# Differential attention: the inner key product step is put between values and scores, the first scores wait for three parts, and weight splits are moved to the last heads

## The chip, the cores and the metric

The kernel runs on one core of a Trainium2 chip. The metric is the device time of one execution in microseconds (us). Three runs of the kernel before gave 1989.1, 1990.81 and 1990.58 us; the median is 1990.58.

## The reference, cut to what matters

The whole program is two transformer blocks on 512 tokens of width 1024. The part that the change touches is the differential attention of the second block:

```python
q = apply_rope(q, cos, sin)          # 8 heads, 2 components of 64
k = apply_rope(k, cos, sin)
s = jnp.einsum('bqhcd,bkhcd->bhcqk', qb, k) * scale      # causal
p = jax.nn.softmax(s, axis=-1)
a = p[:, :, 0] - lam * p[:, :, 1]
o = jnp.einsum('bhqk,bkhe->bqhe', a, v)                  # v: 128 wide
```

Beside it the program computes the first four column tiles of another product of the same normed input (`proj = h @ w_in`): raw keys and values of the compressed branch and the keys of two other branches. This is the "inner key product" here, stage `nsf`.

## The kernel before, in words

Every large product is made exact with three matmuls: high by high, high by low, low by high. Weights come in 512 KB chunks into six slots. For each chunk SyncE loads the raw floats, ScalarE casts them to the high part `Wh` (line 1324), VectorE writes the low part `Wl` over the raw floats (line 1834), and TensorE may then use it. These two instructions are a **weight split**. A chunk's slot comes free when TensorE is done with the chunk five or six places earlier, so a split may be made early or late within that span.

The attention stage has 32 tiles `t`: 8 heads of 4 query tiles each. Tile `t` belongs to head `t // 4`; with `t % 4` from 0 to 3 its scores are 512, 384, 256 and 128 keys wide, so the widest tile of a head comes first. The engines run written-out lists in order; they meet only at semaphores:

- **TensorE** (`attention`, line 893): `scores(0)`, `scores(1)`, eight inner product steps, and then for each `t`: `values(t-2)` (line 867: two matmuls for each 128 keys), `scores(t+2)` (lines 844 to 848, twice, for the components m = 0 and 1), `turn(t)` (line 857: transposes of the combined probabilities), and one inner product step where there is one (`nsf_step(t)`: every `t` below 27 but 0, 9, 18; three matmuls of 512 columns, lines 689 to 691). All inner steps add up in bank 7, a column tile being eight steps.
- **VectorE** (line 2043): for each `t`: `combine(t)` (lines 2036, 2038, 2040: both components of the exponentials into one, which lets `turn(t)` go), `maxima(t+2)` (line 2028, two reductions), and a split where `t` is in `LOW_AT`.
- **ScalarE** (line 1508): for each `t`: at t = 0, 9, 18, 27 `nsf_out` (line 1506: copies bank 7 out and so frees it), `da_out(t-2)` (line 1498, writes YD and frees bank 6 for the next `values`), `turned_out(t)` (line 1494: the transposed tile into ATd, for `values`), `exps(t+2)` (line 1485), at `t % 4` 3 and 0 a `q_high` (line 1533: high part of the next head's queries), and a split where `t` is in `HIGH_AT`.
- **GpSimd** (`qk_low`, line 558): for each head two casts (`Kh`, line 572) and four subtractions that write the low parts: `Kl` m = 0, `Kl` m = 1 (line 579), `Qst` m = 0, `Qst` m = 1 (line 587). Each subtraction adds one to `st_lo`; `scores` of a head's first tile waits for all four. They are fenced by `a_ready` of the head before, and the two last by `q_high`.

Banks 0 to 3 of PSUM hold scores, 4 and 5 transposes, 6 the output, 7 the inner product. At t = 29 to 31 `nst_tile` steps (304 columns wide) of the next product stand behind the turns.

Of the kernel before, what the change touches and what calls it, by code (L numbers as in the profile page):

```python
# [93 lines left out]
def at_least(eng, sem, value):  # L94

    if isinstance(value, int) and value <= 0:
        return
    eng.wait_ge(sem, value)


def program(nc, t, out, stop=None):
# [9 lines left out]
    with ExitStack() as ctx:  # L111
# [3 lines left out]
        def sem(name):  # L115
            return ctx.enter_context(nc.semaphore(name))
# [156 lines left out]
        for c, units in enumerate((3, 2, 2, 2, 3, 2, 2) * 2):  # L273
            s = len(GATE_AT)
            cuts = (0, 4, 8) if units == 2 else ((0, 3, 5, 8) if s % 2 else (0, 3, 6, 8))
            for n in range(units):
# [51 lines left out]
        st_lo = sem("st_lo")  # L328
# [50 lines left out]

        TWIN_AT = {CHUNK0["vda"] + 4: (0,), CHUNK0["vda"] + 7: (1,), CHUNK0["nsf"]: (2, 3), CHUNK0["nsf"] + 1: (4, 5),  # L380
                   CHUNK0["nsf"] + 2: (6, 7)}
        HIGH_AT = (1, 5, 9, 17, 25)
        LOW_AT = (5, 9, 13, 21, 29)

        def qk_parts(head):

            return 4 * head
# [5 lines left out]
        def nsf_ends(t):  # L393

            return t // 9 if t % 9 == 0 and t // 9 < 4 else None

        def nsf_step(t):

            return 8 + t - t // 9 - 1 if t % 9 and t < 27 else None
# [5 lines left out]
        def exists(t):  # L405

            return 0 <= t < TOTAL

        def tile_of(t):
            return 3 - t % 4  # L410

        def width(t):
            return (tile_of(t) + 1) * P
# [268 lines left out]
        def _(pe):  # L682
            def weights(k, it=0):

                pe.wait_ge(w_lo, it * 4 + (k + 1))
                return k % SLOTS

            def three(dst, a_hi, a_lo, b_hi, b_lo, start, stop):
                tensor.matmul(dst, a_hi, b_hi, start=start, stop=False)  # L689
                tensor.matmul(dst, a_hi, b_lo, start=False, stop=False)  # L690
                return tensor.matmul(dst, a_lo, b_hi, start=False, stop=stop)  # L691

            def bank_free(stage, b, k=0):
                at_least(pe, free[b], k + FREED[stage][b])
# [137 lines left out]
            def scores(t):  # L832
                i, u, b2 = tile_of(t), t // 4 % 2, 2 * (t % 2)
                w = width(t)
                q = slice(i * P, (i + 1) * P)
                if t % 4 == 0:
                    pe.wait_ge(st_lo, qk_parts(t // 4) + 4)
                    pe.wait_ge(k_twin[u], 32 * (t // 8) + 32)
                for m in range(2):
                    b = b2 + m  # L840
                    bank_free("da", b, t // 2)
                    dst = ps[b][:, 0:w]
                    if m == 1:
                        tensor.matmul(ps[b][:, w - P:w], identb[:], causal, start=True, stop=False, skip_group_check=True)
                    tensor.matmul(dst, Qst[:, u, m, q], Kh[:, u, m, 0:w], start=m == 0, stop=False, skip_group_check=m == 1)  # L845
                    last = tensor.matmul(dst, Qst[:, u, m, q], Kl[:, u, m, 0:w], start=False, stop=m == 1, skip_group_check=m == 1)
                    if m == 0:
                        last = tensor.matmul(ps[b][:, w - P:w], identb[:], causal, start=False, stop=True)
                    last.then_inc(full[b], 1)

            def turn(t):

                pe.wait_ge(a_ready, t + 1)
                b = 4 + t % 2
                bank_free("da", b, t // 2)
                for j in range(width(t) // P):
                    last = tensor.transpose(ps[b][:, j * P:(j + 1) * P], Pb2[:, t % 2, 0, j * P:(j + 1) * P], ident[:])
                last.then_inc(full[b], 1)

            def values(t):  # L860
                u, n = t % 2, tile_of(t) + 1
                b = 6
                bank_free("da", b, t)
                head = t // 4
                bank_free("da", 4 + u, t // 2 + 1)
                for j in range(n):
                    last = tensor.matmul(ps[b][:, 0:P], ATd[:, u, j * P:(j + 1) * P], vd[:, j, head * P:(head + 1) * P],  # L867
                                         start=j == 0, stop=j == n - 1)
                last.then_inc(full[b], 1)

            def nsf_steps(a, b):
                for n in range(a, b):
                    c, k = n // 8, n % 8
                    w = weights(CHUNK0["nsf"] + c)
                    if k == 0:
                        bank_free("nsf", 7, c)
                    q = slice(k * P, (k + 1) * P)
                    last = three(ps[7][:], Wh[:, w, q], Wl[:, w, q], HTh[:, k, :], HTl[:, k, :], k == 0, k == KT - 1)
                    if k == KT - 1:
                        last.then_inc(w_used, 1)  # L880

            def nst_tile(c, tt):
                s = weights(CHUNK0["nst"] + c)
                q = slice(tt * P, (tt + 1) * P)
                if c == 0:
                    bank_free("nst", tt)
                for j, k in enumerate(range(c * VG_K, min(c * VG_K + VG_K, KT))):
                    n = slice(j * VG_W, (j + 1) * VG_W)
                    last = three(ps[tt][:, 0:VG_W], HTh[:, k, q], HTl[:, k, q], Wh[:, s, n], Wl[:, s, n], k == 0, k == KT - 1)
                if tt == TT - 1:  # L890
                    last.then_inc(w_used, 1)

            def attention():
                scores(0)
                scores(1)
                nsf_steps(0, 8)
                for t in range(TOTAL):
                    if exists(t - 2):
                        values(t - 2)
                    if exists(t + 2):  # L900
                        scores(t + 2)
                    turn(t)
                    if nsf_step(t) is not None:
                        nsf_steps(nsf_step(t), nsf_step(t) + 1)
                    if t == TOTAL - 3:
                        nst_tile(0, 0)
                        nst_tile(0, 1)
                    if t == TOTAL - 2:
                        nst_tile(0, 2)
                        nst_tile(0, 3)  # L910
                    if t == TOTAL - 1:
                        nst_tile(1, 0)
                        nst_tile(1, 1)
                values(TOTAL - 2)
                nst_tile(1, 2)
                nst_tile(1, 3)
                values(TOTAL - 1)
# [175 lines left out]
            if on("da"):  # L1093
                pe.wait_ge(st_zero, 1)
                attention()
# [221 lines left out]
        def _(ac):  # L1317
# [8 lines left out]
            def chunk_done(stage, c, it=0):  # L1326
                ac.wait_ge(w_used, it * 4 + (CHUNK0[stage] + c + 1))

            def filled(stage, b, k=0):
                ac.wait_ge(full[b], k + (FILLED[stage][b] + 1))  # L1330
# [157 lines left out]
            def turned_out(t):  # L1488

                w = width(t)  # L1490
                u = t % 2
                filled("da", 4 + u, t // 2)
                at_least(ac, full[6], FILLED["da"][6] + t - 1)
                scalar.copy(ATd[:, u, 0:w], ps[4 + u][:, 0:w]).then_inc(free[4 + u], 1)
# [6 lines left out]
            def nsf_out(c):  # L1501
                chunk_done("nsf", c)
                if c >= 2:
                    ac.wait_ge(st_lo, qk_parts((4, 7)[c - 2]) + 4)
                dst = kcv[:, c, :] if c < 2 else kraw[:, c - 2, :]
                scalar.copy(dst, ps[7][:]).then_inc(free[7], 1)

            def attention():
                exps(0)
                exps(1)  # L1510
                for t in range(TOTAL):
                    if nsf_ends(t) is not None:
                        nsf_out(nsf_ends(t))
                    if exists(t - 2):
                        da_out(t - 2)
                    turned_out(t)
                    head = t // 4 + 2
                    if exists(t + 2):
                        exps(t + 2)
                    if t % 4 == 3 and head < 8:  # L1520
                        q_high(head, 0)
                    if t % 4 == 0 and 2 <= t // 4 + 1 < 8:
                        q_high(t // 4 + 1, 1)
                    if t in HIGH_AT:
                        split(CHUNK0["vda"] + 7 + HIGH_AT.index(t) + LEAD)
                da_out(TOTAL - 2)
                da_out(TOTAL - 1)
# [299 lines left out]
        def _(ve):  # L1827
# [215 lines left out]
            def attention():  # L2043
                maxima(0)
                maxima(1)
                for t in range(TOTAL):
                    combine(t)
                    if exists(t + 2):
                        maxima(t + 2)
                    if t in LOW_AT:  # L2050
                        split(CHUNK0["vda"] + 7 + LOW_AT.index(t) + LEAD)

# [583 lines left out]
```

## Time and profile before

| | |
|---|---|
| median of three runs | 1990.58 us |
| the profiled execution | 1989.57 us |
| its span | 1987.8 us |
| TensorE (matmul) busy | 1962.2 us, 99% |
| VectorE, ScalarE, GpSimd busy | 52%, 41%, 14% |
| chain of waits | 92% on TensorE |
| granted TensorE clock | full in all slices |

A time in a row counts from the start of the span. TensorE rows are matmuls: the start of one that follows a short matmul is shown up to 0.09 us early, and its end holds the drain of the array (0.16 us and more), so two starts are a better measure than one length. The square brackets say how long the engine sat idle before the row and who released it. Where equal instructions were merged, the row says how many.

### The profile page before, as it was taken

What the parts mean: (1) busy time and instruction counts of PE and PEld (TensorE: products, weight loads), DVE (VectorE), ACT (ScalarE), POOL (GpSimd) and SP (SyncE); (2) the same over time, 40 slices, a digit from 0 to 9 for tenths busy, and PEclk for the clock granted to TensorE, in tenths of its full rate; (3) what the DMA queues carried; (4) which work ended last, traced back from release to release, by engine and by line L of the source; (5) the groups of instructions that cost most, each with busy time, mean ns of one, the idle gap of its engine ahead of it and who ended that gap; (6) DMA issues with size and microseconds to landing.
All of it is one profiled execution on the core that took longest, in us unless ns stands there. A gap on an engine that the chain in (4) does not pass through costs nothing.

```text
span 1987.8 us, 25222 instructions
## 1 busy us (share of the span) xinstructions
PE 1962.2 (99%) x10000; PEld 1662.0 (84%) x10000; DVE 1029.9 (52%) x1575; ACT 805.4 (41%) x1466; POOL 269.6 (14%) x280
## 2 busy tenths in 40 slices
PE   8999999999999999999999999999999999999998
PEld 7888988888888888888988788888888888888887
DVE  6765665555354222333563768877765543222333
ACT  5542543334343222333333873566663342222332
POOL 1001000000000000000003542477860000000000
PEclk9999999999999999999999999999999999999999
DMA  6331333333323333332453144211225323333332
GB/s 213 106 100 56 112 107 102 98 96 96 96 88 107 101 98 96 96 96 85 122 151 114 50 149 148 73 61 49 64 78 198 112 79 110 98 96 95 96 96 74
DMA packets 60100, 201.68 MB, mean 101 GB/s; under 512 B 8304, under 2 KB 8336, under 8 KB 59600
## 3 DMA queue, kind: packets, MB, share of 16 engines
q1 hardware_dynamic: 56080, 185.10, 30.0%
q0 software_dynamic: 3904, 14.97, 2.2%
q8 instruction: 80, 1.31, 0.3%
q14 instruction: 36, 0.29, 0.1%
HBM read 180.64 MB, written 8.39 MB: 95 GB/s over the span
## 4 chain that ended last, share of the span: by engine, by line
PE 92%; DVE 3%; ACT 2%; POOL 1%; issue 1%; DVEq 1%; DMA 1%; POOLq 0%; ACTq 0%; SPq 0%
PE ps L691 27%; PE ps L689 27%; PE ps L690 27%; PE ps L1203 1%; PE ps L1241 1%; PE ps L1240 1%; PE ps L1183 1%; PE ps L1184 1%; PE ps L781 1%; PE ps L1110 1%; POOL PU L645 1%; DVE XN L1874 1%; PE ps L867 1%; ACT XN L1357 0%; PE ps L845 0%
## 5 line engine op out<-in xcount | busy, mean ns | idle before, releaser
L1834 DVE TENSOR_TENSOR Wl<-raw,Wh 128x1024 fp32r<-128x1024 f32 x307 | 378.3, 1235 | 688.9 <-ACT Wh L1324 687.5
L689 PE MATMUL ps<-HTh,Wh 128*128 128x512 f32 (+1 forms) x1712 | 641.4, 375 | 2.1 <-DVE gst L2416 1.2
L691 PE MATMUL ps<-HTh,Wl 128*128 128x512 f32 (+1 forms) x1712 | 636.8, 372 | 0.0
L690 PE MATMUL ps<-HTl,Wh 128*128 128x512 f32 (+1 forms) x1712 | 636.5, 372 | 0.0
L1324 ACT CAST Wh<-raw 128x1024 fp32r<-128x1024 f32 x307 | 321.7, 1051 | 736.1 <-DMA raw<-in_w_all 736.1
L691 PEld LDWEIGHTS ps<-HTh,Wl 128*128 128x128 f32 x1712 | 322.4, 188 | 56.3
L689 PEld LDWEIGHTS ps<-HTh,Wh 128*128 128x128 f32 x1712 | 322.6, 188 | 55.8 <-issue 2.1
L690 PEld LDWEIGHTS ps<-HTl,Wh 128*128 128x128 f32 x1712 | 322.7, 189 | 53.3
L689 PE MATMUL ps<-Wh,Yh 128*128 128x512 f32 x528 | 205.8, 390 | 0.0
L691 PE MATMUL ps<-Wh,Yl 128*128 128x512 f32 x528 | 205.5, 389 | 0.0
L690 PE MATMUL ps<-Wl,Yh 128*128 128x512 f32 x528 | 205.4, 389 | 0.0
L645 POOL TENSOR_SCALAR PU<-PU,ugg 128x512 f32<-128x512 f32 (+3 forms) x128 | 138.6, 1099 | 74.1 <-DVE ugg L2397 74.0
L689 PEld LDWEIGHTS ps<-Wh,Yh 128*128 128x128 f32 x528 | 99.1, 188 | 20.6
L690 PEld LDWEIGHTS ps<-Wl,Yh 128*128 128x128 f32 x528 | 99.1, 188 | 20.5
L691 PEld LDWEIGHTS ps<-Wh,Yl 128*128 128x128 f32 x528 | 99.1, 188 | 20.4
L689 PE MATMUL ps<-Wh,HTh 128*128 128x512 f32 (+1 forms) x288 | 110.7, 384 | 0.0
L691 PE MATMUL ps<-Wh,HTl 128*128 128x512 f32 (+1 forms) x288 | 109.4, 380 | 0.0
L690 PE MATMUL ps<-Wl,HTh 128*128 128x512 f32 (+1 forms) x288 | 109.3, 380 | 0.0
L1753 ACT ACTIVATE PU<-ps,umx 128x512 f32<-128x512 f32 (+3 forms) x128 | 65.9, 528 | 56.0 <-DVE umx L2389 56.0
L593 POOL MEMSET Kl<- 64x512 f32 x4 | 2.0, 522 | 453.6 <-DVE qkd L1943 453.6
L691 PEld LDWEIGHTS ps<-Wh,HTl 128*128 128x128 f32 x288 | 54.1, 188 | 10.1
L690 PEld LDWEIGHTS ps<-Wl,HTh 128*128 128x128 f32 x288 | 54.1, 188 | 9.7
(287 smaller groups left out, 2265.6 us busy)
## 6 DMA issues: line engine op xcount, KB each, us to landing
raw<-in_w_all SPq DMA_DIRECT2D x307, 512.0 KB, 3.5
swp_d<-qkd SPq DMA_DIRECT2D x64, 64.0 KB, 2.8
g_dram<-gst SPq DMA_DIRECT2D x16, 256.0 KB, 3.8
ring<-g_dram POOLq DMA_DIRECT2D x16, 256.0 KB, 3.5
X<-in_x SPq DMA_DIRECT2D x4, 512.0 KB, 6.2
swp_r<-qkr SPq DMA_DIRECT2D x16, 128.0 KB, 3.6
gpre<-in_g_pre POOLq DMA_DIRECT2D x4, 512.0 KB, 3.9
Kh<-Kh SPq DMA_DIRECT2D x16, 128.0 KB, 2.3
```

The lines of the kernel that those rows point to most:

```text
L645: last = pool.tensor_scalar(p, p, ugg[:, s % 2, i:i + 1], None, ALU.mult)
L689: tensor.matmul(dst, a_hi, b_hi, start=start, stop=False)
L690: tensor.matmul(dst, a_hi, b_lo, start=False, stop=False)
L691: return tensor.matmul(dst, a_lo, b_hi, start=False, stop=stop)
L781: last = tensor.transpose(ps[b][:, j * P:(j + 1) * P], XN[:, tt, k * P:(k + 1) * P], ident[:])
L867: last = tensor.matmul(ps[b][:, 0:P], ATd[:, u, j * P:(j + 1) * P], vd[:, j, head * P:(head + 1) * P], start=j == 0, stop=j == n - 1)
L1110: last = tensor.matmul(ps[kv][:, ht * 64:ht * 64 + 62], cw[:, j, ht * P:(ht + 1) * P], cA[:, kv, j, :], start=j == 0, stop=j == 15)
L1183: tensor.matmul(ps[b][:, o:o + w], q, ksh[:, m, g, 0:w], start=first, stop=False, skip_group_check=not first)
L1184: return tensor.matmul(ps[b][:, o:o + w], q, ksl[:, m, g, 0:w], start=False, stop=end, skip_group_check=not first)
L1324: scalar.copy(Wh[:, s, :], raw[:, s, :]).then_inc(w_hi, 1)
L1753: last = scalar.activation(PU[:, (s + 1) % 2, SCORE_AT[i]:SCORE_AT[i] + w], ps[b][:, o:o + w], ACT.Exp, bias=umx[:, s % 2, i:i + 1], accum ...
L1834: vector.tensor_tensor(Wl[:, s, :], raw[:, s, :], Wh[:, s, :], ALU.subtract).then_inc(w_lo, 1)
```

## The change

Four edits, all in the attention stage: on TensorE the inner step of `t` is issued before `scores(t+2)` and `turn(t)`; on ScalarE `nsf_out` is issued after `turned_out(t)`; the first tile of a head waits for three low parts ahead of component 0 and for the fourth ahead of component 1; and the five weight splits go to other tiles.

```diff
-        HIGH_AT = (1, 5, 9, 17, 25)
-        LOW_AT = (5, 9, 13, 21, 29)
+        HIGH_AT = (17, 21, 25, 27, 29)
+        LOW_AT = (18, 22, 26, 28, 30)
...
                 if t % 4 == 0:
-                    pe.wait_ge(st_lo, qk_parts(t // 4) + 4)
                     pe.wait_ge(k_twin[u], 32 * (t // 8) + 32)
                 for m in range(2):
                     b = b2 + m
+                    if t % 4 == 0:
+                        pe.wait_ge(st_lo, qk_parts(t // 4) + 3 + m)
                     bank_free("da", b, t // 2)
...
                     if exists(t - 2):
                         values(t - 2)
+                    if nsf_step(t) is not None:
+                        nsf_steps(nsf_step(t), nsf_step(t) + 1)
                     if exists(t + 2):
                         scores(t + 2)
                     turn(t)
-                    if nsf_step(t) is not None:
-                        nsf_steps(nsf_step(t), nsf_step(t) + 1)
...
                 for t in range(TOTAL):
-                    if nsf_ends(t) is not None:
-                        nsf_out(nsf_ends(t))
                     if exists(t - 2):
                         da_out(t - 2)
                     turned_out(t)
+                    if nsf_ends(t) is not None:
+                        nsf_out(nsf_ends(t))
                     head = t // 4 + 2
                     if exists(t + 2):
                         exps(t + 2)
```

## Rows read from the trace of the kernel before

**Rows 1.** Page, part 1: busy time, share of the span and instructions of each engine.

```profile
PE 1962.2 (99%) x10000; PEld 1662.0 (84%) x10000; DVE 1029.9 (52%) x1575; ACT 805.4 (41%) x1466; POOL 269.6 (14%) x280
```

**Rows 2.** TensorE's waits in 1080 to 1185 us: total, times, longest.

```profile
PE ps L867 <- ACT YD L1498: 1.5, 2, 1.3
PE ps L857 <- DVE Pb L2040: 1.5, 3, 0.7
PE ps L845 <- POOL Qst L587: 0.9, 3, 0.3
```

**Rows 3.** Windows: the ten us behind the stage (length, then busy of each engine).

```profile
1185.00:1195.00 10.00, 10.00 (x55) 8.81 (x54) 7.35 (x12) 9.84 (x20) 8.85 (x11) 1.00 0.90 320
```

**Rows 4.** Timeline of TensorE, one head: scores(16), scores(17), turn(16), values(16), scores(20).

```profile
1133.11 0.50 PE L845 MATMUL ps<-Kh,Qst 128*128 128x512 f32 x1 [0.29 <-POOL Qst L587]
...
1135.82 0.42 PE L845 MATMUL ps<-Kh,Qst 128*128 128x384 f32 x1
...
1138.86 0.66 PE L857 MATMUL ps<-ident,Pb 128*128 128x128 f32 x4
...
1142.15 1.16 PE L867 MATMUL ps<-vd,ATd 128*128 128x128 f32 x8
...
1143.45 0.50 PE L845 MATMUL ps<-Kh,Qst 128*128 128x512 f32 x1
```

**Rows 5.** Timeline of TensorE, start: scores(3), turn(1), values(0), scores(4).

```profile
1098.31 0.31 PE L845 MATMUL ps<-Kh,Qst 128*128 128x128 f32 x1
...
1098.80 0.28 PE L846 MATMUL ps<-Kl,Qst 128*128 128x128 f32 x1
1099.74 0.55 PE L857 MATMUL ps<-ident,Pb 128*128 128x128 f32 x3 [0.66 <-DVE Pb L2040]
...
1100.82 1.05 PE L867 MATMUL ps<-vd,ATd 128*128 128x128 f32 x8
1101.63 0.48 PE L845 MATMUL ps<-Kh,Qst 128*128 128x512 f32 x1
```

**Rows 6.** Timeline of ScalarE, start: nsf_out(0) and turned_out(0).

```profile
1097.50 0.59 ACT L1506 COPY kcv<-ps 128x512 f32<-128x512 f32 x1 [2.99 <-PE ps L691]
1098.59 0.59 ACT L1494 COPY ATd<-ps 128x512 f32<-128x512 f32 x1 [0.50 <-PE ps L857]
```

**Rows 7.** Timeline of ScalarE and TensorE at t = 9 and 10: nsf_out(1), da_out(7), values(8).

```profile
1120.71 0.59 ACT L1506 COPY kcv<-ps 128x512 f32<-128x512 f32 x1
1121.32 0.37 ACT L1498 ACTIVATE YD<-ps,rr 128x128 f32<-128x128 f32 x1
...
1121.74 1.16 PE L867 MATMUL ps<-vd,ATd 128*128 128x128 f32 x8 [1.31 <-ACT YD L1498]
```

**Rows 8.** Timeline of VectorE: combine(3); maxima(16) and combine(15); maxima(20).

```profile
1104.24 0.35 DVE L2040 SCALAR_TENSOR_TENSOR Pb<-Pb,gg 128x128 f32<-128x128 f32 x1
...
1133.95 1.29 DVE L2028 TENSOR_REDUCE nmx<-ps 128x1 f32<-128x512 f32 x2 [0.61 <-PE ps L848]
...
1135.74 0.88 DVE L2040 SCALAR_TENSOR_TENSOR Pb<-Pb,gg 128x128 f32<-128x128 f32 x1
...
1144.30 1.29 DVE L2028 TENSOR_REDUCE nmx<-ps 128x1 f32<-128x512 f32 x2 [2.03 <-PE ps L848]
```

**Rows 9.** Timeline of VectorE and GpSimd: two weight splits and a low part of queries.

```profile
1078.28 1.30 POOL L587 TENSOR_TENSOR Qst<-qkd,Qst 64x512 fp32r<-64x512 f32 x1 [0.16 <-issue]
1078.80 1.86 DVE L1834 TENSOR_TENSOR Wl<-raw,Wh 128x1024 fp32r<-128x1024 f32 x1 [4.73 <-ACT Wh L1324]
...
1120.18 1.22 DVE L1834 TENSOR_TENSOR Wl<-raw,Wh 128x1024 fp32r<-128x1024 f32 x1
1121.31 0.16 DVE L2036 RECIPROCAL rr<-rs 128x2 f32<-128x2 f32 x1
```

**Rows 10.** Timeline of TensorE, last head: turn(28) and turn(29).

```profile
1169.75 0.66 PE L857 MATMUL ps<-ident,Pb 128*128 128x128 f32 x4 [0.23 <-DVE Pb L2040]
...
1171.75 0.55 PE L857 MATMUL ps<-ident,Pb 128*128 128x128 f32 x3 [0.60 <-DVE Pb L2040]
```

## The prediction, written before any run of the changed kernel

> **What bounds the kernel now.** The page's first part comes first: TensorE is busy for 99% of the span, the others for about half or less [rows 1]. So a change of order can only win TensorE's idle time, or add to it. The windows behind the attention stage show it busy for 10.00 of 10 us [rows 3]; the matmul list there is fixed, so what the stage loses or gains goes to the end undiminished. The waits inside the stage are small and short: values for YD, turn for Pb, scores for Qst, 3.9 us together [rows 2]. Starts against starts tell more, since each wait also empties the array.
>
> Then the timeline of one head, read as a loop. scores(16) starts at 1133.11, turn(16) at 1138.86 (5.75 later), values(16) at 1142.15 (3.29 later), scores(20) at 1143.45 (1.30 later) [rows 4]. The first leg runs through VectorE: maxima(16) 0.84 behind the scores, combine(15), then maxima(17) and combine(16) [rows 4, 8]. The second runs through ScalarE: turned_out(16), exps(18), q_high, da_out(15), which frees bank 6. In the third, values(16) takes 0.88 and the rest is the wait for GpSimd's last Qst part. TensorE stands still inside all three legs; the loop, not its own work, sets a head's 10.34 us. So each edit is asked one thing: which leg does it lengthen or shorten?
>
> **The inner step ahead of scores.** The same matmuls, in another order: no service is added. The 1.08 us from turn(1) to values(0) are three transposes of 0.11 and one inner step, so the step is taken as 0.70 [rows 5]. Before, it stood between turn(4h+1) and values(4h), where TensorE waits for da_out anyway; there it is free, and taking it away leaves the hole. Now it stands between values(4h) and scores(4h+4): that leg is 0.88 + 0.70 = 1.58 instead of 1.30. In the first leg the step between scores(4h+4) and scores(4h+5) is replaced by its neighbour: nothing. The exception is t = 18, which has no step: there the leg is 0.88.
>
> **Three parts instead of four.** With 1.58 in the third leg all four parts are there, so this edit is idle, but for t = 18: component 0 starts at 0.88, component 1 half a us later, when the fourth part is there. One head gains. From scores(4) to scores(16) the kernel before took 31.48 [rows 4, 5]; the kernel after takes 3 x (5.73 + 3.29 + 1.58) = 31.80 (5.73: the leg of 5.75, less 0.02 since these scores start without a wait). That is +0.32 although the 0.6 of nsf_out(1), which delayed da_out(7) and so values(8), is gone [rows 7]. From scores(16) to scores(20): 5.73 + 3.29 + 0.88 = 9.90 against 10.34, -0.44.
>
> **nsf_out behind turned_out.** At t = 0 this costs. Before, ScalarE copied bank 7 at 1097.50 and sat idle before turned_out(0) at 1098.59 [rows 6]. Now turned_out(0) goes first and the copy starts at 1099.07, ends at 1099.66. Behind it stands the inner step of t = 1, which needs bank 7 and is now ahead of scores(3) and turn(1). Before, scores(3) was done (0.52 from its rows, less what it overlaps) by the time turn(1) stalled until 1099.74 [rows 5]. Now from about 1099.7 TensorE has to do the step 0.70, scores(3) 0.52, turn(1) 0.33, values(0) 0.88 and the next step 0.70 before scores(4); before it had turn(1), one step and values(0). So +1.22. At t = 9 the copy is done about when the step of t = 10 wants the bank: 0 to 0.1, taken as 0. At t = 18 and 27 it pushes exps(20) and exps(29) by 0.6, which the splits below cover; without them combine(20) and combine(29) have 0.8 us and more of slack.
>
> **The splits.** On ScalarE they stand behind exps(t+2) where it waits for TensorE next; cost 0 there. On VectorE the old places (t = 5, 9, 13, 21) lie in the gap before the next head's maxima: the idle time there is 2.03 without a split and 0.61 with one [rows 8]. So taking them out wins nothing. The new places t = 18, 22, 26 lie behind maxima(4h+4), ahead of combine(4h+3), in the middle of the first leg. One split moves the next instruction by 1.13 (1120.18 to 1121.31) [rows 9]. Bounds for the leg: 0.84 + 1.21 (two maxima) + 1.13 + 0.86 (a combine whose last part takes 0.35) + 2.32 (from maxima(17), which starts as combine(15) ends, to turn(16)) = 6.36; and 7.0 where GpSimd's operations stretch these. The row for that: a combine of the same 128 columns took 0.88 beside GpSimd's Kl, 0.35 alone, and a split that met a Qst of GpSimd took 1.86 instead of 1.22 [rows 8, 9]. A leg of 5.75 already holds the 0.53, hidden as VectorE then waits for scores(4h+5) anyway. I place GpSimd's first Kl right at or across the split, so 6.8 at t = 18, 7.0 at t = 22, and 6.36 at t = 26, where GpSimd has no head left.
>
> From scores(20) to turn(28) the kernel before took 26.30 [rows 4, 10]. After: (6.8 + 3.29 + 1.58) + (7.0 + 3.29 + 1.58) + 6.36 = 29.90, so +3.60.
>
> At t = 28 the split stands between maxima(30) and combine(29), on which turn(29) waited already [rows 10]: +1.13, and up to 0.3 more if ScalarE's half of it, now behind nsf_out(3) and exps(29), is late. I take 1.2. At t = 30 nothing but combine(31) is behind the split, and the 304-column steps cover that.
>
> The Trainium skill, page "SBUF — State Buffer", section "Who interferes with whom", says that a VectorE instruction with two SBUF inputs and a GpSimd instruction that reads SBUF lock each other out for the whole instruction. By that rule the sum stands as it is; without it every split leg is 6.36 and the sum 1.1 lower. By that rule, the trace agrees: 1.86 for 1.22 and 0.88 for 0.35.
>
> **Sum:** 1.22 + 0.32 - 0.44 + 3.60 + 1.2 = **+5.9 us**; between +4.8 (no stretch by GpSimd) and +6.4. The profiled execution would be 1989.57 + 5.9 = 1995.5. It stood 1.0 below the median of the three runs, so the forecast of a median is about 1996.3. A measurement of this kernel can tell 0.2%, or 4.0 us, from no change; the runs before lie 1.7 us apart.
>
> **The rivals.**
>
> *VectorE has slack in the first leg* (0.22). Then the splits of t = 18 to 26 cost nothing and only the start and the legs count: 1.22 + 0.32 - 0.44, and two legs of 1.58 for 1.30, +0.56; the split at 28 is hidden too: +1.7, 1992.2, no change. For it: VectorE is busy 52% over the span [rows 1]. Against: turn(28) and turn(29) were released by Pb with TensorE idle [rows 10], and the head's leg is the sum of VectorE's parts. Also here belongs that two of the terms are half as large as I make them.
>
> *The other side: the holes are filled* (0.12). If ScalarE with two or three splits fewer in the early heads lets da_out go earlier, values(4h) no longer waits, and the inner step fills what was Qst's wait. The waits for Qst (0.42 in the head shown, five such heads [rows 4]) and for YD (1.31 at t = 10 [rows 7], and an estimate of 0.3 in each of five more, the idle start of such a leg) would go: -4.9, 1985.7. It decides where turn(4h) to values(4h) falls below some 2.4 us. Against: that leg is made of turned_out, exps, q_high and da_out, none of which is removed, and the split stood behind them.
>
> *More than I see* (0.06): bank 7 also holds the inner steps of t = 10 and 19, and component 1 waits in other heads: another 0.7 in each of three heads, 1998.4.
>
> *The three-part wait does nothing at all* is part of the forecast for six heads of seven; if it also does nothing at t = 18, 0.4 is to be added.
>
> **How the numbers follow.** The forecast has 0.60. Its low end 1995.3 is above the bound of 1994.6 by less than the legs are certain, so I count 0.04 of it elsewhere, 0.03 as no change and 0.01 as faster. Faster 0.12 + 0.01 = 0.13, same 0.22 + 0.03 = 0.25, slower 0.56 + 0.06 = 0.62. The range must take in the first rival and the whole forecast: 1990.5 to 1998.6; the filled holes and the far end are left out.
>
> **What the changed profile would show.** Right: a wait of TensorE's L689 for ScalarE's L1506 near 1099, of 1 us or more, and scores(4) near 1102.85; no wait of L845 for Qst, or one at t = 20 alone; values(4h) idle for about 1 us before each; heads 1 to 3 at 10.6 us; scores(20) to turn(20) and scores(24) to turn(24) at 6.4 to 7.0; splits of VectorE between maxima and combine, some of 1.8 us; turn(29) 3 us or more behind turn(28). Wrong: turn(4h) at the old distance although the split is there; or values(4h) less than 3 us behind turn(4h).

## The result and the profile after

The kernel after takes 1998.22 us, the median of six runs (1995.61 to 1999.12), against 1989.45 us for six runs of the kernel before: a ratio of 1.0041 [1.0031, 1.005], slower by 8.8 us. The profiled execution took 1998.14 us with a span of 1996.3 us, 8.57 us more than the one of before.

First the page of the kernel after: busy time of each engine.

```profile
PE 1962.7 (98%) x10000; PEld 1663.0 (83%) x10000; DVE 1033.2 (52%) x1575; ACT 805.2 (40%) x1466; POOL 268.5 (13%) x280
```

Against [rows 1] TensorE's busy time is the same within 0.5 us and the span is 8.5 longer. Then TensorE's waits in the stage, 1080 to 1185 us of the kernel after: total, times, longest.

```profile
PE ps L868 <- ACT YD L1499: 5.0, 7, 0.8
PE ps L858 <- DVE Pb L2041: 4.8, 6, 1.3
PE ps L689 <- ACT kcv L1507: 1.3, 1, 1.3
PE ps L689 <- ACT kraw L1507: 0.3, 1, 0.3
```

Beside [rows 2] the wait for Qst is gone, values waits in every head, turn waits six times instead of three, and bank 7 is a new releaser. The sum is 11.4 us against 3.9; the 7.5 between them is not the change's cost, since what the table below shows in its last large row is no wait at all. Starts against starts are the safe measure.

The start of the stage, timeline of TensorE: the step of t = 1, turn(1), values(0), the next step, scores(4).

```profile
1099.50 0.47 PE L689 MATMUL ps<-HTh,Wh 128*128 128x512 f32 x1 [1.25 <-ACT kcv L1507]
...
1100.79 0.51 PE L858 MATMUL ps<-ident,Pb 128*128 128x128 f32 x3
1101.14 1.06 PE L868 MATMUL ps<-vd,ATd 128*128 128x128 f32 x8
1101.96 0.47 PE L689 MATMUL ps<-HTh,Wh 128*128 128x512 f32 x1
...
1102.72 0.40 PE L846 MATMUL ps<-Kh,Qst 128*128 128x512 f32 x1
```

And ScalarE there:

```profile
1098.28 0.59 ACT L1495 COPY ATd<-ps 128x512 f32<-128x512 f32 x1 [4.08 <-PE ps L858]
1098.76 0.59 ACT L1507 COPY kcv<-ps 128x512 f32<-128x512 f32 x1
```

nsf_out(0) now ends at 1099.35, and only then may the step of t = 1 go; scores(4) starts at 1102.72 instead of 1101.63 [rows 5]. Since the stage itself began 0.31 earlier in this execution, that is +1.39.

Two later heads, timeline of VectorE: maxima(20), the split of t = 18, the last part of combine(19); the same for maxima(24).

```profile
1145.22 1.29 DVE L2029 TENSOR_REDUCE nmx<-ps 128x1 f32<-128x512 f32 x2 [0.49 <-PE ps L849]
1146.43 1.22 DVE L1835 TENSOR_TENSOR Wl<-raw,Wh 128x1024 fp32r<-128x1024 f32 x1
...
1148.15 0.79 DVE L2041 SCALAR_TENSOR_TENSOR Pb<-Pb,gg 128x128 f32<-128x128 f32 x1
...
1156.89 1.29 DVE L2029 TENSOR_REDUCE nmx<-ps 128x1 f32<-128x512 f32 x2 [1.17 <-PE ps L849]
1158.09 1.85 DVE L1835 TENSOR_TENSOR Wl<-raw,Wh 128x1024 fp32r<-128x1024 f32 x1
...
1160.44 0.35 DVE L2041 SCALAR_TENSOR_TENSOR Pb<-Pb,gg 128x128 f32<-128x128 f32 x1
```

And GpSimd's first Kl of each of these heads:

```profile
1146.60 2.19 POOL L579 TENSOR_TENSOR Kl<-qkd,Kh 64x512 fp32r<-64x512 f32 x1 [0.25 <-issue]
...
1157.58 1.28 POOL L579 TENSOR_TENSOR Kl<-qkd,Kh 64x512 fp32r<-64x512 f32 x1 [0.25 <-issue]
```

The split stands in the leg from scores to turn, as foreseen. Where it was first, GpSimd's Kl took 2.19; where the Kl was first, the split took 1.85. The legs are 6.78 and 6.88.

The last head, timeline of TensorE: turn(28), values(27), turn(29), the first of eighteen 304-column matmuls, values(28).

```profile
1174.26 0.66 PE L858 MATMUL ps<-ident,Pb 128*128 128x128 f32 x4 [0.74 <-DVE Pb L2041]
1175.58 0.49 PE L868 MATMUL ps<-vd,ATd 128*128 128x128 f32 x2 [0.67 <-ACT YD L1499]
...
1177.92 0.90 PE L858 MATMUL ps<-ident,Pb 128*128 128x128 f32 x3 [1.31 <-DVE Pb L2041]
1178.47 0.60 PE L689 MATMUL ps<-Wh,HTh 128*128 128x304 f32 x1
...
1183.18 1.14 PE L868 MATMUL ps<-vd,ATd 128*128 128x128 f32 x8
```

Three transposes take 0.90 instead of 0.55 [rows 10], and from 1178.47 to 1183.18 pass 4.71 us for 18 matmuls. The windows of the kernel after say why (length; busy time and number for PE, PEld, DVE, ACT, POOL; then the granted clock, the DMA share, GB/s):

```profile
1178.00:1180.00 2.00, 2.00 (x9) 2.00 (x10) 1.09 (x5) 1.14 (x6) 0.51 (x1) 0.50 0.99 229
1180.00:1182.00 2.00, 2.00 (x10) 2.00 (x9) 0.98 (x1) 0.98 (x2) 0.00 (x0) 0.50 0.81 328
```

The same windows of the kernel before:

```profile
1178.00:1180.00 2.00, 2.00 (x18) 2.00 (x17) 0.00 (x0) 0.52 (x2) 0.00 (x0) 1.00 0.92 317
1180.00:1182.00 2.00, 2.00 (x18) 2.00 (x16) 0.00 (x0) 0.00 (x0) 0.00 (x0) 1.00 0.60 240
```

Busy is 2.00 of 2.00 in both, but 9 and 10 matmuls are done instead of 18. The granted clock was 0.50, its level of 1.2 GHz, from 1176.53 for 6.83 us. The page does not show it: its 40 slices of the granted clock read 9 throughout, as before (a 9 stands for 90% or more), and the busy time counts the slow matmuls as work. Only the mean over the span hints at it, 0.997 against 0.999.

Where the 8.9 us came in, by starts counted from the stage's first scores (before 1089.84, after 1089.53):

| | before | after | more |
|---|---|---|---|
| scores(4) | 11.80 | 13.19 | +1.39 |
| scores(4) to scores(16) | 31.47 | 31.85 | +0.38 |
| scores(16) to scores(20) | 10.35 | 9.83 | -0.52 |
| scores(20) to turn(28) | 26.29 | 29.85 | +3.56 |
| turn(28) to turn(29) | 2.00 | 3.66 | +1.66 |
| turn(29) to values(28) | 2.90 | 5.27 | +2.37 |
| values(28) to values(31) | 9.88 | 9.96 | +0.08 |

The column adds to 8.92; less the 0.31 by which the stage began earlier it is 8.61, and the execution is 8.57 longer. The code ahead of the stage is the same in all kernels here, and the stage began anywhere from 1089.46 to 1090.35 in the profiled executions, so the 0.31 is not the change's.

### The profile page after: what moved, and what is told of

The parts are those of the page before. It is cut to its first block, busy times and chain, and to the rows that moved or that the text cites. A ratio compares the mean times of both kernels' runs of the same rounds, so it can differ in the third digit from the quotient of the medians.

```text
span 1996.3 us, 25230 instructions
## 1 busy us (share of the span) xinstructions
PE 1962.7 (98%) x10000; PEld 1663.0 (83%) x10000; DVE 1033.2 (52%) x1575; ACT 805.2 (40%) x1466; POOL 268.5 (13%) x280
## 3 DMA queue, kind: packets, MB, share of 16 engines
q8 instruction: 80, 1.31, 0.3%
## 4 chain that ended last, share of the span: by engine, by line
PE 91%; DVE 3%; ACT 2%; DVEq 1%; issue 1%; DMA 1%; POOL 1%; POOLq 0%; ACTq 0%; SPq 0%
PE ps L689 27%; PE ps L691 26%; PE ps L690 26%; PE ps L1204 1%; PE ps L1242 1%; PE ps L1241 1%; PE ps L1184 1%; PE ps L1185 1%; PE ps L868 1%; PE ps L1111 1%; PE ps L781 1%; POOL PU L645 1%; DVE XN L1875 1%; ACT XN L1358 0%; PE ps L1040 0%
## 5 line engine op out<-in xcount | busy, mean ns | idle before, releaser
L689 PE MATMUL ps<-HTh,Wh 128*128 128x512 f32 (+1 forms) x1712 | 641.4, 375 | 4.6 <-ACT kcv L1507 1.3
L689 PEld LDWEIGHTS ps<-HTh,Wh 128*128 128x128 f32 x1712 | 322.7, 188 | 59.2 <-issue 4.0
L689 PE MATMUL ps<-Wh,Yh 128*128 128x512 f32 x528 | 205.8, 390 | 0.0
L689 PEld LDWEIGHTS ps<-Wh,Yh 128*128 128x128 f32 x528 | 99.1, 188 | 20.4
L689 PE MATMUL ps<-Wh,HTh 128*128 128x512 f32 (+1 forms) x288 | 111.7, 388 | 0.0
```

## The experiments

Ten more runs were made, nine of them of new kernels. In short (times in us; H is turn(4) to turn(28), six heads; A is turn(28) to turn(29); B is turn(29) to values(28); C is how long the granted clock was 0.50 in the stage; H to C are from the one profiled execution of each). A ratio is to the kernel before on the same chip; that kernel's medians there were 1989.68 for the runs from splits only to nsf_out(0) first, 1989.33 for those from split of 28 at 29 to both, and 1989.22 for the last run and the kernel after again.

| kernel | median | ratio to before | H | A | B | C |
|---|---|---|---|---|---|---|
| before | 1989.45 | 1 | 62.40 | 2.00 | 2.90 | 0 |
| after | 1998.22 | 1.0041 [1.0031, 1.005] | 65.89 | 3.66 | 5.27 | 6.83 |
| after, again | 1997.45 | 1.0039 [1.0024, 1.0055] | 65.86 | 3.66 | 4.36 | 6.83 |
| splits only | 1994.54 | 1.0025 [1.0015, 1.0035] | 65.84 | 3.18 | 4.44 | 3.41 |
| three parts only | 1989.24 | 0.9997 [0.9988, 1.0006] | 62.03 | 2.01 | 2.90 | 0 |
| after, old splits | 1992.05 | 1.0011 [1.0002, 1.002] | 63.15 | 2.06 | 2.91 | 0 |
| after, nsf_out(0) first | 1995.81 | 1.0032 [1.0019, 1.0044] | 65.92 | 3.66 | 4.43 | 3.41 |
| after, split of 28 at 29 | 1994.62 | 1.0029 [1.0018, 1.004] | 65.89 | 2.18 | 2.88 | 0 |
| splits outside | 1987.13 | 0.9988 [0.9979, 0.9996] | 60.17 | 1.78 | 2.90 | 0 |
| Kl later | 1988.59 | 0.9994 [0.9985, 1.0003] | 61.05 | 2.01 | 2.90 | 0 |
| both | 1986.06 | 0.9982 [0.9973, 0.9991] | 59.07 | 1.78 | 2.90 | 0 |
| after with filler | 1996.26 | 1.0034 [1.0021, 1.0046] | 66.14 | 3.39 | 2.90 | 0 |

### The parts of the change

**Splits only**, in the kernel before:

```diff
-        HIGH_AT = (1, 5, 9, 17, 25)
-        LOW_AT = (5, 9, 13, 21, 29)
+        HIGH_AT = (17, 21, 25, 27, 29)
+        LOW_AT = (18, 22, 26, 28, 30)
```

> The kernel before with the splits at the new places and nothing else. Theory (the splits lie in the leg from scores(4h) to turn(4h)): scores(20) to turn(20) and scores(24) to turn(24) at 6.4 to 7.0 us, scores(28) to turn(28) near 6.3, turn(28) to turn(29) 3.2 to 3.7; together +4 us, and +2.4 more if the granted clock of TensorE falls in the last head as it does in the changed kernel: 1993.5 to 1996. Rival (VectorE has slack there): within 0.5 us of before.

Measured: 1994.54, about 4.9 above before. The three legs from scores to turn of the late heads are 7.24, 7.23 and 6.35, A grows by 1.18. In the profiled execution the clock fell too, at 1177.45 for 3.41 us, and B grew by 1.54. That execution took 1995.76, the longest of the eight and 6.2 above the profiled one of before: 3.4 in H, 1.2 in A, 1.5 in B. The median stands only 4.9 above before, about what H and A cost, so most of these executions may have had no fall, which no trace shows.

**Old splits**, the counterpart: the kernel after with the first two lines above put back.

> The changed kernel with the splits back at their old places. Theory: the start's +1.4 stays, the inner step between values and scores adds 0.1 to 0.3 per head but at t = 18; no drop of the clock; +2 us, 1991.5. Rival (the inner step itself costs most): 1995 or more.

Measured: 1992.05, 2.4 above before; no fall of the clock. So the other three edits together cost what the start costs (+1.39 at scores(4)) and 0.75 in H. From here to the kernel after it is 6.2 in the medians and 6.6 between the profiled executions: 2.74 in H, 1.60 in A, 2.36 in B. This experiment and the one above agree that the splits' places carry most of the loss. The new place of the inner step was not run by itself. In this kernel's trace values(4h) to scores(4h+4) takes 1.69 where the inner step stands in it, against 1.30 to 1.46 before (but behind t = 8, where it was 0.91), and the leg from scores to turn is 0.1 shorter in five of seven heads.

**Three parts only**, in the kernel before:

```diff
-                    pe.wait_ge(st_lo, qk_parts(t // 4) + 4)
...
+                    if t % 4 == 0:
+                        pe.wait_ge(st_lo, qk_parts(t // 4) + 3 + m)
```

> The kernel before with the three-part wait and nothing else. Theory (the third leg is 0.88 where TensorE does not wait for the fourth part): values(4h) to scores(4h+4) at 0.9 instead of 1.30 to 1.47 in the heads where it waited, five or six of them; -2.6 us, 1987. Rival (component 1 just waits in its place, and maxima with it): no change in the distance from values(4h) to turn(4h+4), 1989.5.

Measured: nothing, 0.9997 [0.9988, 1.0006], a miss. TensorE's wait for Qst is gone and scores(16) starts 0.47 earlier, but turn(16) does not. Timeline of VectorE and GpSimd in this kernel, the same place as [rows 8]:

```profile
1133.83 1.29 DVE L2029 TENSOR_REDUCE nmx<-ps 128x1 f32<-128x512 f32 x2
...
1135.62 1.45 DVE L2041 SCALAR_TENSOR_TENSOR Pb<-Pb,gg 128x128 f32<-128x128 f32 x1
```

```profile
1133.94 0.60 POOL L572 CAST Kh<-qkd 64x512 fp32r<-64x512 f32 x1 [0.44 <-DVE Pb L2041]
1134.78 0.61 POOL L572 CAST Kh<-qkd 64x512 fp32r<-64x512 f32 x1 [0.23 <-issue]
1135.64 1.28 POOL L579 TENSOR_TENSOR Kl<-qkd,Kh 64x512 fp32r<-64x512 f32 x1 [0.25 <-issue]
```

VectorE came 0.5 earlier to the last part of combine(15) and met the whole of GpSimd's Kl instead of its end: 1.45 instead of 0.88 [rows 8], 0.35 alone. So there is a second loop under the one I read: combine(4h+2) lets Kh go (the bracket of the first row), Kh leads to the first Kl, and the first Kl holds up combine(4h+3), behind which VectorE has maxima(4h+5) and combine(4h+4), on which turn(4h+4) waits. A split at 4h+1 delays combine(4h+2) and with it that Kl. Whatever TensorE wins ahead of it is given back there.

### The start

**nsf_out(0) first**, the kernel after with:

```diff
+                    if nsf_ends(t) is not None and t not in (9, 18, 27):
+                        nsf_out(nsf_ends(t))
...
-                    if nsf_ends(t) is not None:
+                    if nsf_ends(t) is not None and t in (9, 18, 27):
                         nsf_out(nsf_ends(t))
```

> The changed kernel with nsf_out(0) ahead of turned_out(0) again, the other three behind. Theory: the wait of 1.3 us for bank 7 goes and scores(4) starts 1.2 to 1.4 us earlier, all else equal: 1996.8; 1994.4 if the clock should not fall in this one. Rival (turn(1) waits for combine(1) anyway): no gain, 1998.2.

Measured: scores(4) at 11.89, within 0.1 of before, so 1.3 of the start's 1.39 is this one order. turn(29) comes 1.28 earlier than in the kernel after. The median is 2.4 lower. Of that 1.3 is the start, and in the profiled executions 0.84 is in B, since the clock fell here for 3.41 us, not 6.83.

### The last head

**Split of 28 at 29**, the kernel after with:

```diff
-        LOW_AT = (18, 22, 26, 28, 30)
+        LOW_AT = (18, 22, 26, 29, 30)
```

> The changed kernel with VectorE's half of the fourth split at t = 29, behind combine(29), instead of t = 28. Theory: turn(28) to turn(29) falls from 3.66 to about 2.0, TensorE is busier in the last head and its granted clock stays at 2.4 GHz behind turn(29), which gives 1.7 + 2.3 us: 1994.2. Rival (the clock fell for the waits of the whole stage, not for the last head): the clock falls all the same, 1996.5.

Measured: 1994.62, 3.6 under the kernel after, for one 1.2 us instruction moved by one tile. H is the same 65.89, A falls by 1.48, B by 2.39. Timeline of TensorE in this kernel: turn(28), values(27), turn(29), values(28).

```profile
1174.65 0.66 PE L858 MATMUL ps<-ident,Pb 128*128 128x128 f32 x4 [0.74 <-DVE Pb L2041]
1175.98 0.49 PE L868 MATMUL ps<-vd,ATd 128*128 128x128 f32 x2 [0.67 <-ACT YD L1499]
...
1176.83 0.52 PE L858 MATMUL ps<-ident,Pb 128*128 128x128 f32 x3
...
1179.70 1.05 PE L868 MATMUL ps<-vd,ATd 128*128 128x128 f32 x8
```

The wait of 1.31 ahead of turn(29) is gone, and in this execution the clock did not fall. That the one follows from the other is not shown: in the second trace of the kernel after, below, the clock fell at 1174.90, ahead of that wait, behind waits that stand in this kernel too (from the head before on, there 0.95, 0.76, 1.03 and 0.75 us up to turn(28), here 0.95, 0.76, 1.02 and 0.74). So the 2.39 in B is what a kept clock gives, but one trace cannot say that this order of work always keeps it. The 1.48 in A is the split: A is 3.66 or 3.67 in the kernel after, in its second trace and with nsf_out(0) first, whether the clock fell before turn(28) had ended or behind the start of turn(29).

**Filler and the kernel after again.** Is it the standing still that costs the clock, or the late arrival? The kernel after was run once more, beside one that has the same waits but fills them: 14 matmuls of 512 columns into the idle bank 7, whose result nobody reads. They are added work.

```diff
+            def filler(n):
+                pe.wait_ge(free[7], FREED["nsf"][7] + 4)
+                for j in range(n):
+                    tensor.matmul(ps[7][:], Wh[:, weights(CHUNK0["nst"]), 0:P], HTh[:, j, :], start=True, stop=True)
...
+                    if t == 29:
+                        filler(4)
                     if exists(t - 2):
...
+                    if t in (28, 29):
+                        filler(5)
                     turn(t)
```

> The changed kernel once more, for a second trace. If the fall of the granted clock belongs to this order of work, it is there again behind turn(28), lasts 3.4 or 6.8 us, and the time is 1998; if it was a chance, the trace has none and the time is 1995.6, as one of the six executions had.

> The changed kernel with 14 more matmuls of 512 columns into the idle bank 7 (nobody reads them): 5 ahead of turn(28), 4 ahead of values(27), 5 ahead of turn(29), 3.1 us of work in all, where TensorE waits for VectorE and ScalarE anyway. Theory (the idle TensorE of the last head lets its clock fall to 1.2 GHz for 6.8 us, and that costs 2.4): the clock stays, the kernel is faster though it does more: 1995.8. Rival (the clock falls for another reason, or the fillers stand in the way): 1998 or more.

Measured on the same chip: 1996.26 (1995.2 to 1996.86) with the filler, 1997.45 (1997.11 to 1997.85) without. The two windows of the kernel with filler, columns as before:

```profile
1178.00:1180.00 2.00, 2.00 (x15) 1.69 (x14) 1.48 (x6) 1.10 (x6) 1.09 (x3) 1.00 0.79 184
1180.00:1182.00 2.00, 2.00 (x18) 2.00 (x18) 0.95 (x1) 1.02 (x2) 0.00 (x0) 1.00 0.72 246
```

In all three executions turn(29) starts 88.37 or 88.38 from the stage's start, as late as ever. With the filler the granted clock stays at 1.00 and B is 2.90, as before the change. In the repeated run the clock fell at 1174.90, again for 6.83 us, and was back at 1181.73, before values(28); so B was 4.36 there, not 5.27, and the kept clock gave 1.46 in B and not the 2.4 expected. Work added to a bounding engine made the kernel 1.2 us faster, and no execution with the filler was as slow as the fastest without. Since turn(29) came as late as ever, lateness is not what costs; TensorE's standing still is what the filler took away. That it always keeps the clock rests on one trace and on these five and four times.

### Can the holes be had?

**Splits outside.** If splits at 4h+1 hold up the second loop, and splits at 4h+2 the first, no place in the middle heads is free. The kernel before with the three-part wait, nsf_out(1) and (3) behind turned_out, and all splits at the ends:

```diff
-        HIGH_AT = (1, 5, 9, 17, 25)
-        LOW_AT = (5, 9, 13, 21, 29)
+        HIGH_AT = {0: (0, 1), 29: (2,), 30: (3,), 31: (4,)}
+        LOW_AT = {0: (0, 1), 30: (2,), 31: (3, 4)}
...
                 exps(1)
+                for n in HIGH_AT[0]:
+                    split(CHUNK0["vda"] + 7 + n + LEAD)
...
                     combine(t)
+                    if t in LOW_AT:
+                        for n in LOW_AT[t]:
+                            split(CHUNK0["vda"] + 7 + n + LEAD)
```

> The kernel before with three-part wait, nsf_out(1) and nsf_out(3) behind turned_out, and no split between t = 1 and t = 29: two splits in the gap of VectorE and ScalarE under the first eight inner steps, three at the end. Theory (a head is paced by GpSimd: its first Kl, which a split at 4h+1 delays, holds combine(4h+3)): turn(4h) to turn(4h+4) at 10.05 in all heads instead of 10.3 to 10.5, -2 us, 1987.4. Rival (the early splits are hidden): 1989.5.

Measured: 1987.13, 0.9988 [0.9979, 0.9996]; a head is 10.03 instead of 10.40 (H through six). The two splits that VectorE makes from 1095.25 cost nothing at the start: scores(4) starts at 11.79, as before.

**Kl later.** The kernel with three parts only, and GpSimd's first Kl fenced behind the combine that it used to hold up:

```diff
-                        if head >= 2 and m == 1:
-                            behind(tile + 1)
+                        if head >= 2:
+                            behind(tile + 1 + m)
```

> The kernel with the three-part wait alone, and GpSimd's Kl for m = 0 and 1 let go by combine(4h+3) and combine(4h+4), one later than before. Theory (in the run with the three-part wait alone the earlier scores were given back because combine(4h+3) took 1.45 us behind a Kl of GpSimd instead of 0.88): combine(4h+3) takes 0.35, turn(4h) to turn(4h+4) falls to about 9.95, -2.5 to -3 us, 1986.8. Rival (the leg is bound by something else, component 1 or scores(4h+5)): 10.4 as before, 1989.3.

Timeline of VectorE in this kernel, the last part of combine(15) and maxima(17):

```profile
1134.92 0.35 DVE L2041 SCALAR_TENSOR_TENSOR Pb<-Pb,gg 128x128 f32<-128x128 f32 x1
1135.73 1.03 DVE L2029 TENSOR_REDUCE nmx<-ps 128x1 f32<-128x384 f32 x2 [0.46 <-PE ps L849]
```

The combine is back at 0.35, so it was the Kl that had stretched it. But only part comes through: 0.46 of the 1.1 goes into a new wait, for scores(17), and TensorE waits for Qst again, twice, 0.3 in all. H is 0.98 shorter than with three parts only, less than half of what I expected, and the median is 0.7 under before, which the interval [0.9985, 1.0003] does not tell from nothing.

**Both.** Splits outside, and Kl later.

> Both edits of the two runs before: splits outside, Kl later, three-part wait, nsf_out(1) and (3) behind turned_out. Theory: 9.9 per head, -3.5 us, 1986; faster than the kernel before by more than the noise. Rival (the two edits reach the same wait): no better than the better one of the two alone.

Measured: 1986.06, 0.9982 [0.9973, 0.9991]. A head is 9.85. This beats both kernels of the case, by 3.3 us on its chip (before: 1989.33). TensorE's waits in the stage of this kernel:

```profile
PE ps L858 <- DVE Pb L2046: 1.7, 3, 0.7
PE ps L868 <- ACT YD L1499: 1.0, 2, 0.8
```

## Why the prediction was right, and where it was not

**The direction and its mechanism were right.** The forecast was slower, by +5.9 in the profiled execution; +8.57 came. The signs named in advance were there: the wait of L689 for L1507 is 1.25, no wait for Qst is left, and turn(29) is 3.66 behind turn(28); only the idle time before values(4h) was 0.7 to 0.8 instead of about 1. Term by term: the start +1.22, measured +1.39; scores(4) to scores(16) +0.32, measured +0.38; scores(16) to scores(20) -0.44, measured -0.52; scores(20) to turn(28) +3.60, measured +3.56, its legs 6.78, 6.88 and 6.24 for 6.8, 7.0 and 6.36. Moving nsf_out(0) alone gave the start back, and the stretched rows (0.79 for 0.35 in the first of the two heads, 1.85 for 1.22 in the second: 0.44 and 0.63 more) make most of the 0.54 and 0.64 that these legs have over the 6.24 of the head without GpSimd.

That the middle terms came out so close is partly luck. The inner step was taken as 0.70; the third leg is 1.69 with it and 0.91 without, so it costs 0.78, and from turn to the next scores it is 4.97 and 4.98, where I had 3.29 + 1.58 = 4.87. The first leg of heads 1 to 4 is 5.63, where I had 5.73. The two misses of 0.1 cancel in each of these heads. The start has two inner steps on its path and nothing to cancel them: 0.16 of the 0.17 by which its term was too small.

**One term was too small.** For turn(28) to turn(29) I took 1.2, with up to 0.3 more if ScalarE's half were late; it is 1.66. Timeline of VectorE of the kernel after, the last 512-key part of combine(28), maxima(30), the split, combine(29):

```profile
1173.45 0.75 DVE L2041 SCALAR_TENSOR_TENSOR Pb<-Pb,gg 128x512 f32<-128x512 f32 x1
1174.12 0.75 DVE L2029 TENSOR_REDUCE nmx<-ps 128x1 f32<-128x256 f32 x2
1175.30 1.23 DVE L1835 TENSOR_TENSOR Wl<-raw,Wh 128x1024 fp32r<-128x1024 f32 x1 [0.43 <-ACT Wh L1325]
...
1177.24 0.62 DVE L2041 SCALAR_TENSOR_TENSOR Pb<-Pb,gg 128x384 f32<-128x384 f32 x1 [0.30 <-issue]
```

ScalarE's half was late by 0.43: 1.13 + 0.43 = 1.56 of the 1.66. I named that lateness, with at most 0.3, and put only 0.07 of it into the sum.

**The step that failed** is "the matmul list there is fixed, so what the stage loses or gains goes to the end undiminished". The list is fixed, its speed is not: 2.37 us more in B and 0.08 behind it came from the granted clock, and the prediction had no term for it. The terms that it had measured +6.47 together, against 5.9. What changed ahead of the fall is in this window of the last head, in the kernel before:

```profile
1165.00:1175.00 10.00, 8.97 (x67) 7.91 (x66) 8.58 (x24) 6.98 (x24) 1.69 (x4) 1.00 0.64 158
```

and after:

```profile
1165.00:1175.00 10.00, 7.36 (x51) 5.64 (x50) 8.24 (x18) 8.05 (x24) 1.85 (x2) 1.00 0.30 89
```

The busy share of such a window does not decide by itself. The same window of splits only, where the clock fell, and of split of 28 at 29, where it did not:

```profile
1165.00:1175.00 10.00, 8.53 (x56) 6.36 (x54) 7.51 (x18) 8.82 (x25) 2.13 (x2) 1.00 0.35 95
1165.00:1175.00 10.00, 7.48 (x55) 5.97 (x54) 8.36 (x19) 8.04 (x26) 1.84 (x2) 1.00 0.26 87
```

I had worked out how long TensorE would stand still, and put the stillness down at its own length only.

**The range held, but not for its own reason.** 1998.22 lies 0.4 under the upper end of 1998.6. The forecast's own bound of +6.4 reaches only 1996.8; the one number of the prediction near 1998.6 is the 1998.4 of the rival of bank 7 and component 1, and the prediction says that this far end is left out. That rival gave 0.3 us (the one wait for kraw), not 2.1. The time came in by luck: the fall of the clock, which no term held, happened to cost about what that rival was priced at. The step from the profiled execution to a median (+0.8) was too large as well: over six runs the median of before is 1989.45, 0.1 under that execution.

**The rivals.** VectorE's slack is refuted by the three legs. The holes were not filled: the wait for YD grew from 1.5 to 5.0. That the three-part wait does nothing in six heads of seven fits the trace: values(4h) to scores(4h+4) is 1.68 to 1.71 in all but the one behind t = 18, where it is 0.91. By itself, in the kernel before, it removed TensorE's wait and still won nothing.

**A reason of mine that was too short:** "taking them out wins nothing", said of the early splits because VectorE was idle behind them. From turn(4) to turn(16), three heads, the kernel before takes 31.51; without the early splits 31.23; with three parts 31.55; with both (the kernel with splits outside) 30.13. Each alone is worth 0.3 or nothing, both together 1.4. Up to 0.6 of that may be nsf_out(1), which that kernel also puts behind turned_out [rows 7]; the rest is more than the sum of the two. The idle time of VectorE was real, but the split also delayed combine(4h+2) and so GpSimd; that this is the whole reason was not tried by itself.

## What to carry to other kernels

Read a head as a loop with legs, and ask of each engine's loop whether a gain upstream only makes it meet the next one earlier: two edits that are worth nothing alone may be worth something together. When an edit makes TensorE stand still near a dense stretch, allow for the granted clock of that stretch too, and look for it in windows with the number of matmuls beside the busy time. For a side task on a loaded engine, look for a place behind the last wait that matters: the split at t = 29 left A at 2.18 against 2.00 before, and one tile earlier A was 1.48 longer, and the kernel 3.6 us slower with what the clock cost.

## What the runs showed of the hardware

In this stage the granted clock fell to 1.2 GHz in four of the profiled executions (the kernel after twice, splits only, nsf_out(0) first), always between 1174.90 and 1177.52, in the last head, where TensorE stood still for 0.2 to 1.3 us at a time between groups of matmuls, and for 3.41 or 6.83 us. At that level a 304-column matmul took 0.253 us from start to start, at 2.4 GHz 0.139. In those of the other kernels it did not fall there. What decides between 3.41 and 6.83, and whether every execution of the kernel after has the fall (one of six took 1995.61, which would fit one without), stays open: only the profiled executions show where the clock fell. Nor is it known which wait brings the fall, since the kernel with the split of 28 at 29 had nearly the same waits up to turn(28) as the kernel after and kept its clock. The Trainium skill, page "TensorE: Matmul & The Clock Gate", section "A second HAM failure mode: psum-queue depth-cycling", says that short but frequent idling of TensorE between groups of matmuls can make its clock change back and forth between the two levels. The traces agree in part: no single wait of the last head was over 1.32 us, but the clock went down once and up once in the stage, not back and forth.

Where VectorE's combine and GpSimd's Kl met, the first took 1.45 for 0.35 and the second its own 1.28; the combine starts 0.02 us earlier in the records and was yet the one that waited. The Trainium skill, page "SBUF — State Buffer", section "Who interferes with whom", says that the order of issue decides who is blocked. Two pairs of the kernel after agree: the split that started 0.17 ahead of a Kl kept its 1.22 while the Kl took 2.19, and the Kl that started 0.51 ahead of a split kept its 1.28 while the split took 1.85. The pair with 0.02 between the starts can't settle it, since GpSimd's times are rough.
